# Gate matrices from one fp32 product per token, an earlier key top-k, 80 expert candidates, and all dots in the gate stage

## The reference, cut to what matters

```python
q = (x @ wq).reshape(T, 8, 2, 128)
s = einsum('thpd,hpkd->thpk', q, sub_keys)          # 8 heads x 2 halves x 128 keys
s_top, i_top = top_k(s, 16)
cand_s = s_top[:, :, 0, :, None] + s_top[:, :, 1, None, :]   # 16 x 16 = 256 candidates
best, pos = top_k(cand_s, 16)
gate = softmax(best)                                # expert index = key0 * 128 + key1
a = gelu(x . u_tab[idx]);  y = sum_k gate * a * v_tab[idx]
```

## Time and profile before

| | |
|---|---|
| median of the runs | 2396.19 us (2393.13 to 2396.74) |
| profiled run | 2387.49 us, its span 2385.5 us |
| PE busy | 2230.2 us, 93% |
| DVE busy | 1659.7 us, 70% |
| POOL busy | 706.4 us, 30% |
| ACT busy | 624.8 us, 26% |
| chain that ended last | PE 57%, DVE 36%, issue 5% |

### The profile page before, as it was taken

How to read it: one execution, slowest core, us unless ns; L and a number is a source line. 1 busy time by engine, 2 the same in 40 slices (tenths; PEclk the granted TensorE clock), 3 DMA queues, 4 the chain that set the end, 5 groups by cost and what they waited for, 6 DMA issues and landing times.

```text
span 2385.5 us, 32711 instructions
## 1 busy us (share of the span) xinstructions
PE 2230.2 (93%) x10332; PEld 1571.6 (66%) x10332; DVE 1659.7 (70%) x4153; ACT 624.8 (26%) x934; POOL 706.4 (30%) x605
## 2 busy tenths in 40 slices
PE   8999999699999999978989898997999999999998
PEld 2554443445998788855555555555788888888886
DVE  4222331623129999999999999994898988666665
ACT  2111022223222222222232233222322222222222
POOL 0000001003224544433343343431565553222220
PEclk9999999799999999999999999999999999999999
DMA  9011134105204544424777756778999999888883
GB/s 351 17 71 71 41 106 146 75 22 185 71 1 146 171 142 145 143 88 148 225 216 214 211 178 199 212 214 250 387 416 383 407 373 359 290 285 294 288 289 149
DMA packets 293500, 475.86 MB, mean 199 GB/s; under 512 B 148871, under 2 KB 150055, under 8 KB 292872
## 3 DMA queue, kind: packets, MB, share of 16 engines
q1 hardware_dynamic: 256520, 340.20, 42.1%
q0 software_dynamic: 36864, 134.23, 15.7%
HBM read 401.76 MB, written 72.61 MB: 199 GB/s over the span
## 4 chain that ended last, share of the span: by engine, by line
PE 57%; DVE 36%; issue 5%; DMA 1%; ACT 1%; SPq 0%; DVEq 0%; POOL 0%; ACTq 0%
PE ps L950 29%; DVE eA L1418 13%; PE ps L617 5%; PE ps L825 3%; PE ps L707 3%; DVE junk L1388 3%; PE ps L628 3%; PE ps L860 2%; PE ps L861 2%; PE ps L673 2%; DVE eB L1416 2%; DVE oneh L1340 1%; PE ps L616 1%; PE ps L888 1%; DVE sidx L1312 1%
## 5 line engine op out<-in xcount | busy, mean ns | idle before, releaser
L888 PE MATMUL ps<-h2hi,uhi 128*128 128x512 f32 x1024 | 446.1, 436 | 23.8 <-issue 18.2
L950 PE MATMUL ps<-vhi,whi 128*128 128x512 f32 x1024 | 400.1, 391 | 23.4 <-DVE wlo L1441 23.4
L888 PE MATMUL ps<-h2hi,ulo 128*128 128x512 f32 x1024 | 404.0, 395 | 0.0
L888 PE MATMUL ps<-h2lo,uhi 128*128 128x512 f32 x1024 | 401.0, 392 | 0.0
L950 PE MATMUL ps<-vlo,whi 128*128 128x512 f32 x1024 | 399.6, 390 | 0.0
L950 PE MATMUL ps<-vhi,wlo 128*128 128x512 f32 x1024 | 399.3, 390 | 0.0
L1418 DVE TENSOR_SCALAR eA<-iota_b,cur 128x128 bf16<-128x128 bf16 x1536 | 395.5, 325 | 0.0
L1797 POOL DMA_INDIRECT ugat<-in_u_rows,idx x128 | 173.4, 1354 | 449.0 <-DVE dots L1388 447.5
L1718 ACT ACTIVATE vhi<-vraw 128x1024 fp32r<-128x1024 f32 x128 | 135.9, 1061 | 474.0 <-PE ps L950 455.1
L1439 DVE TENSOR_TENSOR vlo<-vraw,vhi 128x1024 fp32r<-128x1024 f32 x128 | 156.5, 1223 | 131.3 <-ACT vhi L1718 131.3
L1805 POOL DMA_INDIRECT vgat<-in_v_tab,idx x128 | 152.1, 1188 | 313.8 <-DVE y L1451 267.8
(11 more groups left out here) (272 smaller groups left out, 3000.3 us busy)
## 6 DMA issues: line engine op xcount, KB each, us to landing
uraw<-in_u_t SPq DMA_DIRECT2D x128, 512.0 KB, 4.8
vraw<-in_v_tab SPq DMA_DIRECT2D x128, 512.0 KB, 5.3
gelu_scratch<-aout SPq DMA_DIRECT2D x128, 256.0 KB, 2.6
gate_scratch<-gst SPq DMA_DIRECT2D x16, 2048.0 KB, 13.9
ain<-gelu_scratch SPq DMA_DIRECT2D x128, 256.0 KB, 5.3
gin<-gate_scratch SPq DMA_DIRECT2D x128, 256.0 KB, 5.7
wring<-in_w_ada SPq DMA_DIRECT2D x12, 2048.0 KB, 7.9
wring<-in_w_in SPq DMA_DIRECT2D x6, 2048.0 KB, 8.3
```

The source lines that it names most:

```text
L888: last = pe.matmul(ps[:, b % 4, :], w[:, b % 2, k, :], h[:, k, LP:T], start=(k == 0 and j == 0), stop=(k == KD - 1 and j == 2))
L950: last = pe.matmul(ps[:, y_bank(t) + h, :], w[:, b, (t - 1) * P:t * P], v[:, b, h * 512:(h + 1) * 512], start=(start and j == 0), stop=(st ...
```

## The change

- `BLK_A` goes from 60 to 40, so the last part of the first products has 24 blocks instead of 4; `POOL_FROM` goes from 20 to 8. The loads of the second stage are asked for at block `BLK_C + 4` instead of `BLK_C`.
- Each token's gate matrix is one product of two fp32 one-hots. DVE builds eA (one operation) for every token and eB for every fourth; POOL builds eB for the other three. The gate value is not split any more, so the six small operations a tile for that (L1365 to L1370) go.
- The top 16 keys of tiles 0 to 3 (`T_EARLY` = 4) are found beside the query stage, behind the copies of each half head's scores. Tile 4 follows in the first stage, behind the experts of tile 0.
- The experts are picked out of 80 candidates: pairs of ranks (a, b) in a staircase (`CAND`), which hold every pair that can be in the top 16. Four sums build them, and some nine more small operations turn a position back into ranks.
- All 128 dots are done in the gate stage, two a block (`DOTS_B` = 2), with two gathers a block; the second stage has none.

```diff
-BLK_A = 60
+BLK_A = 40
-U_HEADS_B = NTD
-POOL_FROM = 20
+DOTS_B = 2
+DOTS_IT = DOTS_B * NB_B
+POOL_FROM = 8
+T_EARLY = 4
+POOL_ROWS = TB - TB // 4
+CAND = [(0, 2, 16), (2, 2, 8), (4, 4, 4), (8, 8, 2)]
+NCAND = sum(na * nb for _, na, nb in CAND)
+def dve_row(q):
+    return q % 4 == 3
...
-        eB = at("eB", 122, [P, RING, 128], BF16)
-        eA = at("eA", 124, [P, 3, RING, 128], BF16)
-        eBp = at("eBp", 134, [P, 2, 4, 128], BF16)
+        eA = at("eA", 122, [P, RING, 128])
+        eB = at("eB", 126, [P, 2, TB, 128])
...
-                if n == BLK_C:
+                if n == BLK_C + 4:
...
-                        row = eBp[:, b % 2, q % 4] if quad % QB == 1 else eB[:, q % RING]
-                        for j in range(3):
-                            last = pe.matmul(o_, row, eA[:, j, q % RING], start=(j == 0), stop=(j == 2))
-                        last.then_inc(onehot_used, 1)
+                        pe.matmul(o_, eB[:, b % 2, k], eA[:, q % RING], start=True, stop=True).then_inc(onehot_used, 1)
...
+            def best_keys(t, h):
+                s_ = scores[:, t, h]
+                v_, i_ = sval[:, t, h], sidx[:, t, h]
+                seq(dve.max(v_[:, 0:8], s_))
+                seq(dve.match_replace(srep[:], v_[:, 0:8], s_, NEG))
+                dve.max_index(i_[:, 0:8], v_[:, 0:8], s_)
+                seq(dve.max(v_[:, 8:16], srep[:]))
+                seq(dve.max_index(i_[:, 8:16], v_[:, 8:16], srep[:]))
...
+            dve.wait_ge(h2lo_ready, NT)
             for h in range(HP):
                 up, us = f"sc{h}p", f"sc{h}s"
                 wait_unit(dve, up)
                 dve.tensor_copy(scores[:, 0, h], bank(up, 0, NKEYS)).then_inc(drain_of(up), 1)
                 wait_unit(dve, us)
                 dve.tensor_copy(scores[:, 1:NT, h], bank(us).rearrange("p (t n) -> p t n", n=NKEYS)).then_inc(drain_of(us), 1)
-            wait_drained(dve, f"sc{HP - 1}p")
-            wait_drained(dve, f"sc{HP - 1}s")
+                wait_drained(dve, up)
+                wait_drained(dve, us)
+                for t in range(T_EARLY):
+                    best_keys(t, h)
             wait_gate_rows(1)
...
+            best_experts(0)
+            seq(dve.scalar_tensor_tensor(work[:, 9], selw[:, 0, 0], float(NKEYS), selw[:, 0, 1], ALU.mult, ALU.add))
+            dve.tensor_copy(idx0[:], work[:, 9]).then_inc(idx_ready, 1)
+            for t in range(T_EARLY, NT):
                 for h in range(HP):
+                    best_keys(t, h)
+            for t in range(1, NT):
+                best_experts(t)
...
-                        if (q // 4) % QB != 1:
-                            dve.tensor_scalar(eB[:, s], iota_b[:], cur[:, 1, q:q + 1], None, ALU.is_equal)
-                        for j in range(3):
-                            last = dve.tensor_scalar(eA[:, j, s], iota_b[:], cur[:, 0, q:q + 1], cur[:, 2 + j, q:q + 1],
-                                                     ALU.is_equal, ALU.mult)
-                        last.then_inc(onehot_ready, 1)
+                        if dve_row(q):
+                            dve.tensor_scalar(eB[:, b % 2, k], iota[:], cur[:, 1, q:q + 1], None, ALU.is_equal)
+                        dve.tensor_scalar(eA[:, q % RING], iota[:], cur[:, 0, q:q + 1], cur[:, 2, q:q + 1],
+                                          ALU.is_equal, ALU.mult).then_inc(onehot_ready, 1)
...
-                    dot(it, b, first)
+                    for e in range(DOTS_B):
+                        dot(it, DOTS_B * b + e, first)
...
-                for q in range(4):
-                    col = 4 * (QB * b + 1) + q
-                    pool.tensor_scalar(eBp[:, b % 2, q], iota_b[:], jcur[:, col:col + 1], None, ALU.is_equal
-                                       ).then_inc(onehot_j_ready, 1)
+                for k in range(TB):
+                    if not dve_row(TB * b + k):
+                        pool.tensor_scalar(eB[:, b % 2, k], iota[:], jcur[:, TB * b + k:TB * b + k + 1], None, ALU.is_equal
+                                           ).then_inc(onehot_j_ready, 1)
```

## The result

The changed kernel takes 2329.44 us (median of 4 runs, 2324.43 to 2341.11), the kernel before 2394.66 us on the same chip (4 runs, 2392.3 to 2396.74): a ratio of 0.9735, with a 95% interval of 0.9697 to 0.9773. The profiled run of the changed kernel took 2328.15 us with a span of 2326.4; the span of before was 2385.5. So 59.1 us are to be found in the traces, where 65.8 were forecast.

A forecast was written before the change was run, and what follows sets the result against it. PE nearly always busy, but held up by DVE in gate blocks, the top-k and a 20.3 us gap. Steps sum to 900.5 us against 966.3; minus 65.8 from the 2396.19 median gives 2330 us, range 2300 to 2372.

The forecast's parts named there:

- entry: PE's first expert block waits for head 15's score copies behind head 14's top-k steps: loss 5.6 us, 1.7 for lower clock.
- first stage: 40 expert blocks ahead of the gate stage, top-k off the path: 230.1 us against 347.4 for 60 blocks.
- gate stage, own pace: PE sets the pace at 7.92 us a block, DVE and POOL fitting beside it: 64 blocks, 506.9 us.
- gate stage, losses: PE's losses where the loop jumps back, standing with no wait shown and then at 1.2 GHz, stay: 12 us.
- last 24 blocks: Between gates and second stage: 137.3 us, with 5 us lost to the fifth block's load queued behind a gate store.
- joint: PE's gap ahead of the second stage, with loads asked for earlier: 6.9 us against 22.3, gain 15.4 us.
- A token's product: Gate stage on PE: one fp32 product, 0.20 us plus 0.11 for change of form, costs 0.31 us a token.
- rival (b): POOL and DVE exclude each other: gate block 11.9 us, 2585 us, slower than before; 6%.
- Dots out of the second stage: DVE falls there from 88% to about 75%, but PE had no idle time, so the gain is nothing.
- (a): DMA sets the gate stage: another gather a block, 27 us come back, 2358 us; 13%.
- (c): The fp32 weight loads are exposed on PE: gate blocks of 9.2 us, 2412 us; 4%.
- (d): Top-k ends later than block 37 or new stalls add up; half the gain remains, 2363 us; 9%.

The follow-up runs named there:

- edit (1): Changed kernel with last two key heads' top-k steps behind all score copies, run with two other edits (later first gathers, earlier fifth-block load): 2311.93 us, ratio 0.9669.
- the run of the product alone: Kernel before with only one fp32 product per token's gate matrix; GpSimd's four rows, one dot a block and 60 blocks ahead kept: 2286.0 us, ratio 0.9564.
- the doubled run: Changed kernel with each token's gate product issued twice in place, same operands: 2396.21 us (one run).

## Why the prediction was right, and where not

The number and the range held, but two terms of the sum were off by 35 us and more, in opposite directions, and the mechanism forecast for the gate stage was not the one that set its pace. That the result came within 1 us is luck: GpSimd's own work of 8.0 us a block, which the forecast did not have as a limit, happens to lie next to the 7.92 us that it gave to PE. From the earlier trace rows on, in us:

| Step | forecast | measured |
|---|---|---|
| entry | 7.3 | 5.75 + 1.6 = 7.4 |
| first stage | 230.1 | 239.6 |
| gate stage, own pace | 506.9 | 469.1 |
| gate stage, losses | 12.0 | 47.2 |
| last 24 blocks | 137.3 | 137.4 |
| joint | 6.9 | 4.2 |
| sum | 900.5 | 904.9 |

PE also left the query stage 2.3 us later in this run (711.01 for 708.67); with that the sum gives the span.

- **Entry: right**, by its mechanism too. The copies of head 15 stood behind four steps of head 14 (717.56), and edit (1) took it all back.
- **A token's product: mis-sized,** 0.31 forecast, 0.236 measured, 38 us over the stage. I had added a price for the change of form to the 0.20 of the earlier trace rows. The row alone was nearly right: a second product costs 0.22.
- **Losses of the gate stage: the step that failed.** "So PE sets the pace" rested on 1.4 us of slack for GpSimd, to 0.87 us a comparison. That slack stood against a block of 7.92 us. At the true 7.33 it reached only to 0.78 us a comparison, and rows took 0.845 and gathers 1.23 plus their gap: 8.0 us, more than PE's block by either count. So GpSimd set the pace. The fp32 form was not the error (0.630 us a row in the run of the product alone). I priced the comparison from rows that stood beside one dot a block and had weighed the lock of rival (b) as all or nothing. It is neither: each split or dot of DVE that overlaps GpSimd's rows adds about 0.9 us to them, and the second dot is one more of these.
- **"These stay, 12 us": right in size,** 11.4 us at the three jumps, so that the blocks between them lost the other 36. But it is no fixed cost: in the run with one dot two jumps cost some 0.6 us each and the first nothing. GpSimd does not hold them up (its last row of the pass ended at 1204.99, 8.5 us ahead of DVE's copy). DVE pauses there for 3.0 and 3.4 us, and for 1.6 us with one dot; why it pauses longer is not shown.
- **First stage: right but for two sizes.** Indices at 763 for 757, top-k end at 937 for 919. The later start is 2.3 us of that. The rest is the lock of the earlier trace rows, but not in DVE's ten long products of a one-hot with the key numbers: they took 3.33 us in the mean, 2.29 undisturbed, and 3.34 in the kernel before, so the forecast had that. It is in the short operations, priced at 0.3 us, of which the 80 candidates need more: beside GpSimd's splits some took up to 2.5 us, 19 us in all over their undisturbed lengths, against 3 before. None of it was on the path; the stall at block 8 became 9.4 us for 3, and the chain ahead of the gate stage 6.3 for 4.5.
- **Last 24 blocks: right,** by the mechanism named: the load behind the gate stores left at 1495.56, 19.3 us after the stage's end (20.3 forecast), and ACT waited 7.01 us for it.
- **Joint: right,** 2.13 us for 2.3. DVE's first sum did wait 3.17 us for its gather, but PE did not lose the 2.6 us forecast for that.
- **Dots out of the second stage: right that it gains nothing.** What I did not weigh is that the same dots then cost 45 us where they went.
- **Rivals.** (a), the transfers, decides little in the changed kernel (halved gathers: 8 us). The next limit, once GpSimd is relieved, is not their bytes but SyncE's queue behind the 2 MB stores: with 1 MB stores the same bytes cost 482.8 us, not 534.7. (b) came out in part, at 8.1 us a block, where it does not turn the sign. The Trainium skill (SBUF — State Buffer, "Who interferes with whom") says that an operation of DVE with two inputs from SBUF contends with a GpSimd operation that reads SBUF; the trace agrees, at 0.92 us for each such operation of 1.2 to 1.3 us. (c) fell: weight loads stayed hidden in the doubled run. (d) fell too: the top-k was ready before ACT came to it.

Open is why the second 2 MB store of a pair holds SyncE for 10 to 15 us in some passes and for 6 to 7 in others, why the late loads of U grow when GpSimd is relieved, and what DVE's pause at the jumps is.

## What to carry to other kernels

When a change takes the engine off the path that bounds a stage, price every other engine of that stage against the new, shorter period, not against the old one or against a padded one; here an error in one's favour (a cheaper product) ate the slack of another step. Work moved out of a stage where it was free must pay where it lands: 64 dots that cost the second stage nothing cost the gate stage 45 us. And an edit that shows no gain may uncover a second limit: rows shared four and four made the gate stage 18 us longer, small stores changed nothing, and both together took 34 us off it.

## What the hardware showed

- GpSimd's comparison of 128x128 fp32 took 0.59 us with DVE at rest and 0.630, 0.760, 0.847 and 0.958 us in the mean in four gate stages (product alone, one dot, the changed kernel, four rows with small stores). Each DVE operation of 1.2 to 1.3 us on two SBUF inputs beside it adds about 0.9 us; one-input sums of the same length add nothing that can be seen (0.60 us for the 97 rows beside them). Halving the gathers' bytes changes nothing (0.843).
- An fp32 product of 128 columns between fp32r products costs PE 0.22 to 0.24 us, less than the 0.26 of three bf16 ones.
- A store of gate matrices holds the queue of its issuing engine: in the changed kernel the DMA behind a 2 MB store of SyncE stood 6 to 15 us in issue in all cases but two, and with 1 MB stores 9 us at most, often under 1.
- DVE's operations are held by GpSimd's as well: a short one of 0.23 to 0.3 us on 128x128 took up to 2.5 us beside a GpSimd split of 2.4 (first stage of the changed kernel).
